# The 256th largest indexer score per query: bisection over its bits with counting compares, in place of MAX8 and MATCH_REPLACE rounds

## The reference

```python
score = jnp.einsum('bqh,bqhs->bqs', wib, jax.nn.relu(dots))
admissible = key_chunk <= c
score = jnp.where(admissible[None, None, :], score, -jnp.inf)
_, sel = lax.top_k(score, topk)          # topk = 256
valid = admissible[sel]
...
logits = logits - slopes[None, :, None, None] * dist[:, None]
logits = jnp.where(valid[:, None], logits, -jnp.inf)
p = jax.nn.softmax(logits, axis=-1)
```

## Time and profile before

| | |
|---|---|
| time, median of 3 runs | 2151.42 us (2150.36 to 2153.04) |
| span of the profiled execution | 2145.9 us |
| PE busy | 1971.3 us, 92% |
| DVE busy | 1138.3 us, 53% |
| ACT busy | 532.4 us, 25% |
| POOL busy | 624.0 us, 29% |
| mean granted clock of PE | 0.95 |
| chain that ended last | PE 76%, DVE 16%, issue 3%, ACT 3%, POOL 2% |
| MAX8 (L1552) | 161.1 us in 192 |
| MATCH_REPLACE (L1556) | 166.6 us in 192 |

### The profile page before, as it was taken

One profiled execution on the slowest core, in us unless ns is written; L12 is line 12 of the kernel. 1 busy time (PEld: TensorE's weight loads), 2 busy tenths in 40 slices (PEclk: granted clock), 3 DMA queues, 4 the chain that ended last, 5 costly groups with the idle time before them and its releaser, 6 DMA issues.

```text
span 2145.9 us, 29023 instructions
## 1 busy us (share of the span) xinstructions
PE 1971.3 (92%) x11577; PEld 1641.2 (76%) x11577; DVE 1138.3 (53%) x1689; ACT 532.4 (25%) x1084; POOL 624.0 (29%) x368
## 2 busy tenths in 40 slices
PE   6999999999978889799988877799999999999999
PEld 5887788788867788688777755678777787778777
DVE  4388899997666666566546223622333222322323
ACT  5366521111012223365502242310001100011000
POOL 4222234333323320100023300334333433334341
PEclk9999999999988886899999888899999999999999
DMA  7201011222210003000121100111111111111111
GB/s 230 72 20 30 23 46 50 74 84 89 79 41 2 2 2 118 11 1 1 37 82 40 50 20 0 40 40 49 39 41 47 49 49 49 31 57 49 49 39 78
DMA packets 111954, 102.45 MB, mean 48 GB/s; under 512 B 5051, under 2 KB 99310, under 8 KB 111598
## 3 DMA queue, kind: packets, MB, share of 16 engines
q1 hardware_dynamic: 109550, 92.68, 14.0%
q10 hardware_dynamic: 2304, 8.39, 1.0%
HBM read 87.42 MB, written 13.63 MB: 47 GB/s over the span
## 4 chain that ended last, share of the span: by engine, by line
PE 76%; DVE 16%; issue 3%; ACT 3%; POOL 2%; DMA 1%; DVEq 0%; ACTq 0%; POOLq 0%
PE ps L1167 7%; PE ps L1169 7%; PE ps L1168 7%; PE ps L387 5%; PE ps L388 5%; PE ps L389 5%; PE ps L362 5%; PE ps L363 5%; PE ps L364 5%; PE ps L1031 3%; PE ps L1052 3%; DVE top L1552 3%; PE ps L827 3%; DVE cacc L1567 2%; DVE score L1556 2%
## 5 line engine op out<-in xcount | busy, mean ns | idle before, releaser
L637 POOL TENSOR_TENSOR WS<-WR,zero 128x1024 fp32r<-128x1024 f32 (+1 forms) x119 | 230.1, 1934 | 1250.7 <-PE ps L389 576.0
L639 POOL TENSOR_TENSOR WS<-WR,WS 128x1024 fp32r<-128x1024 f32 (+1 forms) x119 | 296.0, 2487 | 9.3
L402 DVE TENSOR_TENSOR X<-X,ps 128x512 f32<-128x512 f32 x272 | 184.1, 687 | 175.4 <-PE ps L389 170.4
L1167 PE MATMUL ps<-HS,WS 128*128 128x512 f32 x704 | 274.9, 390 | 1.7 <-DVE HS L315 1.7
L1169 PE MATMUL ps<-HS,WS 128*128 128x512 f32 x704 | 274.6, 390 | 0.0
L1168 PE MATMUL ps<-HS,WS 128*128 128x512 f32 x704 | 274.6, 390 | 0.0
L362 PE MATMUL ps<-HS,WS 128*128 128x512 f32 (+1 forms) x656 | 261.4, 398 | 8.7 <-ACT raw L1266 3.9
L363 PE MATMUL ps<-HS,WS 128*128 128x512 f32 (+1 forms) x656 | 257.9, 393 | 0.0
L364 PE MATMUL ps<-HS,WS 128*128 128x512 f32 (+1 forms) x656 | 257.6, 393 | 0.0
L1826 DVE TENSOR_TENSOR prod<-sil,ps 128x512 f32<-128x512 f32 x44 | 28.3, 684 | 419.1 <-PE ps L1169 419.1
L1556 DVE MATCH_REPLACE8 score<-top,score 128x1024 f32<-128x1024 f32 (+2 forms) x192 | 166.6, 875 | 0.0
(11 more groups left out here) (273 smaller groups left out, 3052.9 us busy)
## 6 DMA issues: line engine op xcount, KB each, us to landing
WR<-in_w_gu SPq DMA_DIRECT2D x44, 512.0 KB, 3.8
WR<-in_w_in SPq DMA_DIRECT2D x36, 512.0 KB, 3.7
WR<-in_w_down SPq DMA_DIRECT2D x22, 512.0 KB, 3.5
dsa_spill<-cacc ACTq DMA_DIRECT2D x12, 512.0 KB, 2.6
X<-in_x SPq DMA_DIRECT2D x4, 1024.0 KB, 9.3
KW<-in_w_xkv SPq DMA_DIRECT2D x8, 512.0 KB, 4.9
WR<-in_w_out SPq DMA_DIRECT2D x8, 512.0 KB, 3.5
X<-in_x SPq DMA_DIRECT2D x1, 4096.0 KB, 13.9
```

The source lines that it names most:

```text
L637: pool.tensor_tensor(hi, w, bc(zero1[:, 0:1], [P, cols]), ALU.add).then_inc(w_hi, 1)
L639: pool.tensor_tensor(lo, w, hi.bitcast(F32), ALU.subtract).then_inc(w_split, 1)
L1167: pe.matmul(ps[:, b0 + half, :], lo, HS[:, 0, k, c], start=(k == 0), stop=False)
```

## The change

The 96 rounds go. In their place a 32-bit integer per query is built from the top bit down, the threshold `thr`: the largest value that at least 256 scores reach. For a bit, six counting compares, one per tile 2 to 7, compare the tile's scores with the candidate `cand` and sum the hits through the instruction's accumulator output into `count` (the elementwise result goes to a scratch of bytes, `over`). Then three instructions over 128x6 values set the bit where the count is at least 256 (`keep`, `thr`) and form the next candidate (`cand`). Every one of these waits for the one before (`toplink`); of the six compares only the last is waited for.

One bit stands behind the conv of each of the 12 units, two at each step `v` = 0 to 9 of DVE's projection loop; none is left for the DeltaNet stage. The scores stay as they are, so `logit_bias` must form the mask from `thr`: larger than the threshold, or equal and early enough in a running count of the equal ones (a scan). It has eight instructions for a tile of 384 or more keys where it had two, and stands now at `v` = 9 (tiles 0 to 2, before `rs` and `rq`), `v` = 10 (3, 4), `v` = 11 (5, 6, ahead of the first `unit_norms`) and `v` = 12 (7).

```diff
-PAIRS = [(7, 2), (6, 3), (5, 4)]
-ROUNDS = TOPK // 8
+RANKED = [t for t in range(TT) if (t + 1) * P > TOPK]
+NR = len(RANKED)
+BITS = 32
...
+        over = at("over", [P, 4 * D], cur[0], U8)
...
-        top8 = small("top8", 16)
+        thr = small("thr", 8, I32)
+        cand = small("cand", 8, I32)
+        count = small("count", 8)
+        keep = small("keep", 8, I32)
...
+        over2 = at("over2", [P, 4 * P], cur[0], U8)
...
+        tieA = at("tieA", [P, SEQ], 186)
+        tieB = at("tieB", [P, SEQ], 190)
...
+            clink(dve.memset(cand[:, :], 0))
             clink(dve.memset(raw[:, 0, 0:3], 0.0))
             clink(dve.memset(raw[:, 1, 0:3], 0.0))
 
-            taken = [0]
-
-            def top_rounds(count):
-
-                for i in range(taken[0], min(taken[0] + count, len(PAIRS) * ROUNDS)):
-                    ts = PAIRS[i // ROUNDS]
-                    for k, t in enumerate(ts):
-                        if i:
-                            dve.wait_ge(topk, 4 * i - 1 + k)
-                        dve.max(top8[:, 8 * k:8 * k + 8], score[:, EOFF[t]:EOFF[t + 1]]).then_inc(topk, 1)
-                    for k, t in enumerate(ts):
-                        dve.wait_ge(topk, 4 * i + 1 + k)
-                        s = score[:, EOFF[t]:EOFF[t + 1]]
-                        dve.match_replace(s, top8[:, 8 * k:8 * k + 8], s, TAKEN).then_inc(topk, 1)
-                    taken[0] = i + 1
+            ranked = [0]
+            top_n = [0]
+
+            def toplink(ins):
+                top_n[0] += 1
+                ins.then_inc(topk, 1)
+                dve.wait_ge(topk, top_n[0])
+
+            def top_bit(k):
+
+                for q, t in enumerate(RANKED):
+                    c = (EOFF[t] - EOFF[RANKED[1]]) if q else 0
+                    ins = dve.tensor_scalar((over if q else over2)[:, c:c + (t + 1) * P], score[:, EOFF[t]:EOFF[t + 1]], cand[:, q:q + 1].bitcast(F32),
+                                            0.0, ALU.is_ge, ALU.add, accum_out=count[:, q:q + 1])
+                toplink(ins)
+                if k == 0:
+                    toplink(dve.tensor_scalar(thr[:, 0:NR], count[:, 0:NR], float(TOPK), 1.0, ALU.is_ge, ALU.subtract))
+                else:
+                    toplink(dve.tensor_scalar(keep[:, 0:NR], count[:, 0:NR], float(TOPK), None, ALU.is_ge))
+                    toplink(dve.scalar_tensor_tensor(thr[:, 0:NR], keep[:, 0:NR], BITS - 1 - k, thr[:, 0:NR],
+                                                     ALU.logical_shift_left, ALU.bitwise_xor))
+                if k + 1 < BITS:
+                    toplink(dve.tensor_scalar(cand[:, 0:NR], thr[:, 0:NR], 1 << (BITS - 2 - k), None, ALU.bitwise_xor))
+
+            def top_bits(n):
+
+                for k in range(ranked[0], min(ranked[0] + n, BITS)):
+                    top_bit(k)
+                ranked[0] = min(ranked[0] + n, BITS)
+
+            def logit_bias(t):
+
+                n = (t + 1) * P
+                s = score[:, EOFF[t]:EOFF[t + 1]]
+                nd = negdist[:, (TT - 1 - t) * P:SEQ]
+                if n <= TOPK:
+                    clink(dve.tensor_copy(s, nd))
+                    return
+                q = RANKED.index(t)
+                T, above, tie = thr[:, q:q + 1].bitcast(F32), gB[:, 0:n], tieA[:, 0:n]
+                clink(dve.tensor_scalar(above, s, T, 0.0, ALU.is_gt, ALU.add, accum_out=count[:, q:q + 1]))
+                clink(dve.tensor_scalar(count[:, q:q + 1], count[:, q:q + 1], -1.0, float(TOPK), ALU.mult, ALU.add))
+                clink(dve.tensor_scalar(tie, s, T, None, ALU.is_equal))
+                clink(dve.tensor_tensor_scan(tieB[:, 0:n], bc(ones1[:, 0:1], [P, n]), tie, 0.0, ALU.mult, ALU.add))
+                clink(dve.scalar_tensor_tensor(tie, tieB[:, 0:n], count[:, q:q + 1], tie, ALU.is_le, ALU.mult))
+                clink(dve.tensor_tensor(above, above, tie, ALU.add))
+                clink(dve.tensor_scalar(above, above, 1.0, BIG, ALU.subtract, ALU.mult))
+                clink(dve.tensor_tensor(s, above, nd, ALU.add))
 
...
-                top_rounds(2)
+                top_bits(1)
...
-                top_rounds(3)
+                if ranked[0] < BITS:
+                    top_bits(2)
+                    if ranked[0] == BITS:
+                        for t in range(3):
+                            logit_bias(t)
+                elif v - 10 < 3:
+                    for t in range(3 + 2 * (v - 10), min(5 + 2 * (v - 10), TT)):
+                        logit_bias(t)
...
-                    if b:
-                        top_rounds(1)
...
-                    top_rounds(1)
...
-            def logit_bias(t):
-
-                s = score[:, EOFF[t]:EOFF[t + 1]]
-                nd = negdist[:, (TT - 1 - t) * P:SEQ]
-                if (t + 1) * P <= TOPK:
-                    clink(dve.tensor_copy(s, nd))
-                else:
-                    clink(dve.tensor_scalar(s, s, TAKEN, -BIG, ALU.is_gt, ALU.mult))
-                    clink(dve.tensor_tensor(s, s, nd, ALU.add))
-
             def dsa(part, e0, e1):
-                if part == "top":
-                    top_rounds(2)
-                elif part == "on":
-                    top_rounds(len(PAIRS) * ROUNDS)
+                if part == "on":
                     scale_o(0, 0, T_ON)
-                elif part == "sq":
-                    for t in range(e0 // 2, e1 // 2):
-                        logit_bias(t)
```

More of the change, by code:

```diff
@@ L17 @@
 F32R = mybir.dt.float32r
+I32 = mybir.dt.int32
+U8 = mybir.dt.uint8
 ALU = mybir.AluOpType
@@ L97, in build_layer, with small @@
         cur = [0.0]
-        def small(name, cols):
-            t = at(name, [P, cols], cur[0])
+        def small(name, cols, dt=F32):
+            t = at(name, [P, cols], cur[0], dt)
             cur[0] += (cols * 4 + 31) // 32 * 32 / KB
```

## The result

The changed kernel takes 2165.03 us in the median of 4 runs (2160.53 to 2166.84), beside 2150.89 (4 runs) for the kernel before on the same chip: a ratio of 1.0059, with a 95% interval of 1.0045 to 1.0073. That is 14.1 us slower, where 7.2 were forecast. The profiled execution has a span of 2164.8 us, 18.9 more than before's. So of the 5.5 us that stand above as lying around before's span only some 1.7 do; the other 3.8 say that the profiled execution of the kernel before was faster than its median.

The account below looks back on a forecast made before the run. PE bounds the conv and projection stages, a ring of engines the DeltaNet stage. Terms -2.0 + 17.6 + 1.6 - 10.0 = +7.2 on a 2145.9 us span, with 5.5 around it, gave 2158.6 us, range 2134 to 2184.

Parts of the forecast that it names:

- the stall behind `rq`: Behind PE's unit 13, PE waits for `n0`, the first `unit_norms` multiplication: +17.6 us, plus 1.6 of slow clock; chance 0.5.
- Price of one bit, 5.9 us: On DVE, six counting compares at the MAX8 rate take 5.26 us, three small instructions 0.66; bounds 3.9 and 6.7.
- Small instructions wait for POOL: DVE's `keep`, `thr`, `cand` and most of the bias wait until POOL's split ends; its pair takes 4.4 us each period.
- Conv stage, -2.0: At the last conv, PE waits 1.4 us instead of 3.4 and still loses its clock: -2.0 us.
- Projection stage, `rq` "just in time": Bits end at 531.2, `rq` at 536.6 after bias of tiles 0 to 2; PE's unit 12 ends at 537.2.
- Bias of tiles 3 to 6, 24 us and 8 of waits: Ahead of the first `unit_norms`, DVE needs 24 us plus 8 for two POOL split pairs, giving `n0` at 569.3.
- Tile 7's bias is hidden: In the projection stage, its 8 us lie beside PE's unit 14 and cost nothing.
- DeltaNet stage, -10: Removing thirty rounds gives 2.7 us in block 0 and 2.4 in each of three other blocks: -10 us.
- the danger that I had named: In the DeltaNet stage, PE's clock of 0.85 might change; 0.05 over 237 us would be worth the whole gain.
- Rival 2: POOL's splits hold small instructions much less, so PE has no wait before `unit_norms`: 2136 us; chance 0.2.
- Rival 3: A bit costs 6.7 us, so PE waits longer in the conv and projection stages: 2188 us; chance 0.2.
- Rival 4: Compares run at the fast rate, a bit costs 3.9 us and all bits end before 500: 2139 us; chance 0.1.

Follow-up runs that it names:

- run 6: Changed kernel with compares that write no accumulator, so no counts are made and `thr` stays 0: 2143.96 us, ratio 0.9987.
- run 5: Changed kernel with `cand` and `keep` moved to a free PSUM bank, nothing else changed: 2156.41 us, ratio 1.0016.
- run 1: Changed kernel, same instructions reordered: `rs` and `rq` right behind the last bit, each `unit_norms` ahead of the bias: 2153.39 us, ratio 1.0024.
- run 4: Kernel before with the 30 rounds inside the DeltaNet stage left out (66 of 96 run): 2134.72 us, ratio 0.993.
- run 2: Changed kernel with a two-instruction bias per tile at the same places, without the choice among equal scores: 2134.87 us, ratio 0.9941.
- run 7: Run 3 with `cand` and `keep` in PSUM, also without the choice among equal scores: 2121.43 us, ratio 0.9874.
- run 8: Changed kernel with norms first, `cand` and `keep` in PSUM and a six-instruction bias, tiles in run 1's order: 2142.37 us, ratio 0.9958.
- run 9: Run 8 with another order of the tiles' bias, tile 7 ahead of the last `unit_norms`: 2136.82 us, ratio 0.995.
- run 3: Changed kernel with a two-instruction bias, back in its old DeltaNet-stage place, without the choice among equal scores: 2130.82 us, ratio 0.9921.

## Why the prediction was right, and where it was off

The side and the size of the stall behind `rq` were forecast, and so was the gain in the DeltaNet stage. The forecast had +7.2 us and the change has +13.4. The 6.2 between them are 10.4 for a wait for `rs` that was put at nothing, less 1.9, 0.7 and 1.6 by which the conv stage, the stall at `n0` and the DeltaNet stage came out better. The sum for the stall at `n0` was right partly by luck, as said at its place.

- **Price of one bit, 5.9 us: right.** From 289.89 the six compares take 5.32 us to the start of `keep` (forecast 5.26), and the three small ones 0.2 each in cadence: 5.94. The compare has the rate of MAX8 with 57 ns more at 1,024 elements and 68 at 384, and its read of 83 ns lies beside the next compare. Run 6 shows that the other rate is that of the form without accumulator. The trace agrees with the rule cited from the Trainium skill, "SBUF — State Buffer", section "Who interferes with whom".
- **Small instructions wait for POOL: right,** by one row of 0.82 us ahead of the run, and shown by run 5, which took their waits away by moving two tiles.
- **Conv stage, -2.0: right side, 1.9 short.** PE waits 1.18 instead of 3.40 (forecast 1.4). That it "still loses its clock" failed: after 1.2 us PE still had it.
- **Projection stage, `rq` "just in time": this step failed.** The bits were to end at 531.2, or 533.0 with the 1.8 by which the whole trace is later; they ended at 537.0. Twenty bits took 129.3 us: 118.8 and 10.5 of waits, where I had 6.7. The 0.9 a period was right from 453 us on (`keep` takes 1.02 instead of 0.17 each time); the first two pairs cost 3.6 and 1.2. Behind them the bias of tiles 0 to 2 took 7.8 us, not 4.4, since the scan met a split (2.98 us for 384 elements). So `rq` came 5.8 us late from the bits and 3.4 from the bias, against 0.6 of slack. A plan with almost no slack and its terms near their least was not the likeliest case. It cost 8.46 + 1.9. Run 5 shows the share of the bits' waits: without them PE does not wait for `rs`.
- **Bias of tiles 3 to 6, 24 us and 8 of waits: the sum right, both terms off.** From `rq` to `n0` DVE took 31.3. Without POOL the four tiles would take 27.4: the scan goes at half the rate that I gave it, 1.225 us for 512 elements and 2.29 for 1,024, or 2.08 ns an element. The waits were 3.8, not 8, since only one pair of splits fell into the stretch (at 562.20; the one before it at 537.34): the splits follow PE's units, and PE stood. That 31.3 came out near the 32 forecast is luck. PE waited 15.59 instead of 17.6, with 2.9 of slow clock instead of 1.6 (2.75 of it in the next 32 broadcasts).
- **Tile 7's bias is hidden: right.** PE's first product of the DeltaNet stage waits 0.8 us, as before. In run 1, which moved it behind the last norms, it is part of PE's wait of 15.8.
- **DeltaNet stage, -10: right, with its parts.** -11.6 from the trace, and -13.2 for the time of run 4, where only these rounds are missing. Block 0 gave 2.8 (43.06 us to 40.24, forecast 2.7). In block 2 the fourth of PE's products with the mask waited 1.98 for it and now waits 0.25: the 1.75 of the forecast. The first such product waited 1.71 for DVE's `TTm` and now 1.42 for the mask, and a wait of 1.2 for `TTm` fell to 0.8. That is 2.4 for the block, as forecast, and blocks 1 and 3 show the same waits. The other 1.6 us lie in small waits and in 1.1 us less of PE's busy time. The granted clock was 0.82 in both kernels, so the danger that I had named, another clock in this stage, did not come here; it came in other runs, most in 2, 6 and 7. PE's first and fourth product in block 2 (the first before, then both after):

```profile
712.15 1.15 PE L921 MATMUL ps<-TTm,gam 64*64 64x64 f32 x32 [1.71 <-DVE TTm L1653]
```

```profile
733.37 1.96 PE L931 MATMUL ps<-TTm,gam 64*64 64x64 f32 x32 [1.42 <-POOL gam L725]
...
754.00 1.15 PE L931 MATMUL ps<-TTm,gam 64*64 64x64 f32 x32 [0.25 <-POOL gam L725]
```

Who PE waited for in this stage, first before, then after:

```profile
PE ps L921 <- POOL gam L715: 7.7, 4, 2.0
...
PE ps L921 <- DVE TTm L1653: 5.2, 3, 1.7
PE ps L941 <- DVE TTm L1661: 4.9, 4, 1.4
...
PE ps L921 <- DVE TTm L1661: 1.5, 3, 0.6
```

```profile
PE ps L931 <- POOL gam L725: 6.4, 7, 1.4
...
PE ps L951 <- DVE TTm L1708: 3.1, 4, 0.8
```

- **Rival 2** (no wait of PE) is what the bits and the bias would do without waits for POOL and with a light bias; run 7 is the nearest to it, and lies 15 us under its 2136, of which 11.7 are the shorter DeltaNet stage at a clock of 0.88. **Rival 3** fell with the price of the bit. **Rival 4** had the effect of POOL wrong: run 6 came to 2144, near its 2139, but through a wait of 13.2 in the conv stage that it had not named, and 11.3 in the DeltaNet stage that came with the clock.

So the loss of 13.4 us is 28.9 of PE's two waits and the slow clock behind them, made by a bias of eight instructions and by small ones that wait for POOL, less 3.9 in the conv stage, where a bit is shorter than two rounds, and 11.6 in the DeltaNet stage, where the rounds no longer stand on the path.

## What to carry to other kernels

Price an added instruction not by its elements but by its form: whether it can run beside the other engine that works in SBUF, and where in that engine's period it will fall. Where GpSimd is busy and a PSUM bank is free, try the small tiles of a chain of tiny instructions there: here it took the waits from all 93. When work moves off one stage, count what its successor (here the mask made from a threshold) costs in the stage that receives it, and give a step that comes out "just in time" the price of coming late. Before filling an idle gap, look at what the instructions behind it will then run beside. And when a new version is faster in a stage that was not changed, look at that stage's clock before taking the gain as the version's.

## What the runs showed of the hardware

- The same products, copies and masks of the DeltaNet stage took 292.8, 292.9, 292.9 and 292.8 us at a granted clock of 0.82 (after, runs 1, 5, 8), 290.3 and 290.5 at 0.83 (runs 4, 9), 288.1 at 0.84 (run 3), 281.6 and 281.5 at 0.86 (runs 2, 6) and 281.1 at 0.88 (run 7, which has 10 us more of DVE's work in it). PE was busy 255.6 us in the first kind and 241.8 in the last. This is worth as much as the 30 rounds, and what decides it stays open; a wait of PE ahead of the stage alone does not (the kernel before and run 7 have none, and 0.82 and 0.88). Each of these is one profile.
- The clock differs between executions of one kernel as well. Of run 5's twelve, nine took 2154.7 to 2157.9 us with a mean granted clock of 0.944 or 0.945, and three 2142.8 to 2145.6 with 0.952 to 0.954. Of run 2's nine, six took 2128.3 to 2135.1 (0.953 to 0.956) and three 2140.8 to 2143.9 (0.948 or 0.949). The changed kernel's four lie at 2160.5 to 2166.8, with 0.943 to 0.946. So the 0.86 or 0.88 of one profile is not a fixed property of its kernel, and a median of a few executions can be some 10 us off by it. Whether the DeltaNet stage makes the difference between such executions is not shown: each kernel has one trace.
- A wait of 1.2 us left PE's clock up, one of 3.4 did not the earlier trace rows. After 2.1, 3.9, 5.8, 8.5, 15.6 and 19.0 us the next 32 broadcasts took 3.84, 5.44, 6.53, 5.47, 6.48 and 6.75 us instead of 3.73 (runs 1, 6, 2, after, after, 5): the loss does not grow steadily with the wait.
- The blocking is mutual: POOL's splits of 2.39 us took up to 3.27 when DVE's compares without accumulator (run 6) ran beside them, and up to 3.20 when the bias did (run 9).
- An accumulator read on DVE is an instruction of 83 ns, and the next compare starts with it.
